# A joined tile of sparse weights, and modulation blocks spread unevenly over a projection

## The chip, the cores and the metric

The kernel runs on one core of a Trainium2 chip. The metric is the device time of one execution in microseconds (us). Engines are named as in the profile: PE is TensorE's matmul, PEld its weight load, DVE is VectorE, ACT is ScalarE, POOL is GpSimd, SP is SyncE, which issues the DMAs.

## The reference, cut to what matters

The kernel computes three layers of a sequence model on 512 tokens (256 context, 256 latent) of width 1024. The change lies in the first, "even" mixer, whose features come out of one projection:

```python
gq, gk, gv, gg, mq, mk, mv, mo, mg = _split(h @ w_in, EVEN_SIZES)     # 256 256 512 512 512 512 512 512 16
log_a = [log_sigmoid((h @ a1[d]) @ a2[d] + ab[d]) / GLA_TAU for d in range(2)]      # a1[d]: 1024 x 16
qk = silu(dwconv1d(concat([mq, mk]), conv_w, conv_b))
gates = (mg + gate_b).reshape(bsz, t, 4, ML_HEADS)
'li_f': gates[:, :, 0], 'lf_f': log_sigmoid(gates[:, :, 1])
'li_b': gates[:, :, 2], 'lf_b': log_sigmoid(gates[:, :, 3])
```

`h` is the normalised and modulated input. The modulation is `silu(c) @ mod_w[layer] + mod_b[layer]`, 6 x 1024 values for each layer and each of two conditions. The decays `log_a` go into a gated linear attention (GLA), q, k, v and gates of the second kind into an mLSTM.

## The kernel before

**Weights.** All weights stream through one ring of 5 slots in SBUF. A block is 8 tiles of 128x128 f32, 512 KB. `STREAM` (L109) is the order of the blocks, and SP's queue loads them in that order (`load_weights`, L248): slot i is loaded again when block i-5 is released. A product block is split into a high part (ACT, L493) and a low part (DVE, L498), kept in 3 buffers each (`PARTS`); each tile product is then 3 matmuls. A part's buffer is free when PE has used it up, so ACT makes part e+3 when item e is done, and DVE follows.

**Modulation blocks** (`Modulator.block`, L761) are not multiplied on PE. DVE multiplies each with the two conditions and sums (L769, twice for each block); that also releases its ring slot. DVE does such a block just before the low part of the product block that follows it in `STREAM` (`low_parts`, L587). 28 of them, m16 to m43, lie in the stage at hand.

**The stage `even_in`** (`even_projection`, L1267) has 31 items, each a bank of 512 columns with 8 tiles, so one block for each item. Item 0 is the low-rank decay input (`low`, 32 of 128 columns used), 1 to 4 are gq and gk, 5 to 8 gv, 9 and 10 are the gates `li` and `lf` (8 of 128 columns used in each), 11 to 18 mq and mk with their convolution on DVE, 19 to 22 mv, 23 to 26 gg, 27 to 30 mo. The items of gv, mv and mo are rounds of four that share their blocks; items 0 to 2 run together. PE may use 4 banks for items, so item e+4 waits until ACT has emptied item e.

**Beside them** runs the GLA (`GlaSteps`, L1329), in the other 4 banks. Its steps are written as generators, one for each engine, and each `yield` names a tick, two for each item: an engine takes the step up when its own walk through the items comes to that tick. Every step stands in the engine's one order of instructions, so what it waits for holds up all that is behind it. The ticks:

```python
DECAYS, DIAGONAL, LEVELS, SPACING = 6, 11, 13, 4
SUMS, KEYS, STATES, OUTPUTS, END = 41, (44, 46), (48, 50, 52), (54, 56), 61
```

At DECAYS PE multiplies `low` with `a2` (L1461), DVE clamps the result (L1608), ACT takes absolute value, exponential and logarithm (L1550 to L1553), DVE joins them (L1614). ACT empties item 4 only behind that. Seven levels of 4 ticks follow: distances on PE (L1452), an exponential on ACT, factors on DVE, scores on PE (L1443), taken over by DVE (L1604). SUMS are the last distances. KEYS makes decayed keys. STATES sums three states on PE (L1508); DVE copies them (L1666) and steps them (L1669), and between does the mLSTM gates' sums and peaks (L1740, L1749), on which PE's transposes of the gates wait (L1766) by way of ACT (L1760). OUTPUTS multiplies (L1527), ACT squares (L1579), DVE reduces (L1680) and, at tick OUTPUTS[1]+3, scales (L1686). At END PE transposes (L1539) and DVE applies the gate (L1693). On an even tick of item e, DVE takes the step up behind item e's low parts, on the odd tick after them and any convolution. 12 idle matmuls on PE (`tail`) close the stage; a barrier follows.

Of the kernel before, what the change touches and what calls it, by code (L numbers as in the profile page):

```python
# [22 lines left out]
ACT = mybir.ActivationFunctionType  # L23
AX = mybir.AxisListType

P = 128
D = 1024
KD = D // P
# [8 lines left out]
KF = FF // P  # L37
# [4 lines left out]
MH, MD = 4, 128  # L42
# [18 lines left out]


SEGMENTS = [
    ("mod0", 48 * KD), ("mod1", 48 * KD), ("even_in", 31 * KD), ("even_out", 8 * 8), ("up0", 2 * KF * KD),
    ("down0", 8 * KF), ("ssd_in", 41 * KD), ("ssd_out", 8 * KI), ("up1", 2 * KF * KD), ("down1", 8 * KF),
    ("in2", 85 * KD), ("branch2", 8 * 4 * KB), ("out2", 8 * KD),
]
# [20 lines left out]
def spread_among(few, many):  # L88

    out, placed = [], 0  # L90
    for i, b in enumerate(many):
        while placed < len(few) * (i + 1) // len(many):
            out.append(few[placed])
            placed += 1
        out.append(b)
    return out
# [2 lines left out]
MOD_FIRST = 16  # L99
MOD_PE = 4  # L100
SQUARES_AT = 2
MOD_EVEN = 44
MOD_DOWN = 27
MOD_ODD = 42
# [2 lines left out]
MOD_SSD = 25  # L107

STREAM = spread_among(blocks_of("mod0")[:MOD_PE], blocks_of("mod0")[MOD_PE:MOD_FIRST]) + blocks_of("even_in")[:TOGETHER] \  # L109
    + spread_among(blocks_of("mod0")[MOD_FIRST:MOD_EVEN], blocks_of("even_in")[TOGETHER:]) \  # L110
    + blocks_of("even_out")[:TOGETHER] + spread_among(blocks_of("mod0")[MOD_EVEN:], blocks_of("even_out")[TOGETHER:]) \
    + blocks_of("up0") + blocks_of("down0")[:DOWN_FIRST] \
    + spread_among(blocks_of("mod1")[:MOD_DOWN], blocks_of("down0")[DOWN_FIRST:]) \
# [3 lines left out]
for _name in ("up1", "down1", "in2", "branch2", "out2"):  # L117
# [4 lines left out]

COLUMNS = [
    ("mod_b0", 48), ("mod_b1", 48), ("mix_g0", 8), ("mix_g1", 8), ("ffn_g0", 8), ("ffn_g1", 8), ("final_g", 8),
    ("conv_w0", 9 * 44), ("conv_w1", 9 * 44), ("conv_b0", 44), ("conv_b1", 44), ("low_one", 1),
    ("ml_conv_w", 24), ("ml_conv_b", 8), ("gla_norm", 4), ("ml_norm", 4), ("ml_li_b", 1), ("ml_lf_b", 1),
    ("ssd_conv_w", 72), ("ssd_conv_b", 24), ("ssd_d", 16), ("ssd_norm", 16), ("ssd_dt_b", 1), ("ssd_a_log", 1),
    ("norm2", 8), ("qn_a", 1), ("kn_a", 1), ("qn_c", 1), ("kn_c", 1), ("b_forget", 1), ("lru_conv_w", 16),
    ("lru_conv_b", 4), ("b_rg_a", 4), ("b_rg_x", 4), ("lam", 4), ("cmp_pos", 32),
# [997 lines left out]
def setup(K, modulator, f, a2):  # L1127


    nc = K.nc  # L1130
    filled, loads, tokens, ones, rooted = K.counts(5)
    sums = SumSquares(K, 0, False)
    on_tensor, blocks = blocks_of("mod0")[:MOD_PE], blocks_of("mod0")[MOD_PE:MOD_FIRST]
    modulator.plan_tensor(on_tensor)
    modulator.plan(blocks)

    with nc.Block() as block:  # L1137
        @block.gpsimd
        def _(pool):
            link = Link(pool, filled)  # L1140
            for i, v in enumerate((EPS, 1.0, 0.0)):
                link(pool.memset(K.small[:, i:i + 1], v))
            pool.memset(K.ones[:], 1.0).then_inc(*ones.up())
            for a, v in ((K.ident, 0.0), (K.tri_f, 1.0), (K.tri_b, 1.0)):
                link(pool.memset(a[:], v))
            link(pool.affine_select(out=K.ident[:], in_=K.ident[:], compare_op=ALU.not_equal, fill=1.0, base=0,
                                    pattern=[[-1, P]], channel_multiplier=1))
            link(pool.affine_select(out=K.tri_f[:], in_=K.tri_f[:], compare_op=ALU.is_ge, fill=0.0, base=0,
                                    pattern=[[1, P]], channel_multiplier=-1))
            link(pool.affine_select(out=K.tri_b[:], in_=K.tri_b[:], compare_op=ALU.is_ge, fill=0.0, base=0,  # L1150
                                    pattern=[[-1, P]], channel_multiplier=1))

        @block.sync
        def _(sync):
            modulator.load(sync)
            sync.dma_start(K.cols[:], K.dram["columns"]).then_inc(*loads.up(16))
            sync.dma_start(a2[0:49, :], K.dram["gla_a2"]).then_inc(*loads.up(16))
            load_weights(K, sync, 0)
            sync.dma_start(K.x[:], K.dram["tokens"]).then_inc(*tokens.up(16))
            load_weights(K, sync, MOD_FIRST)  # L1160
            sync.wait_ge(*tokens.at(16))
            sync.wait_ge(*loads.at(32))

        @block.scalar
        def _(act):
            modulator.silu(act)
            for k in range(KD):
                sums.square(act, k, tokens.at(16))
            act.wait_ge(*sums.summed.at(KD))
            rsqrt(act, Link(act, rooted), f["lf"], K.sum_squares(0), K.small[:, 0:1], 1.0 / D)  # L1170

        @block.tensor
        def _(pe):
            for b in on_tensor[:SQUARES_AT]:
                modulator.sum(pe, b)
            pe.wait_ge(*ones.at(1))
            for k in range(KD):
                sums.add(pe, k)
            for b in on_tensor[SQUARES_AT:]:
                modulator.sum(pe, b)  # L1180

        @block.vector
        def _(dve):
            for b in blocks:
                modulator.block(dve, PLACE[b], b)
            dve.wait_ge(*loads.at(16))
            modulator.end(dve, blocks)
            modulator.take_sums(dve, MOD_PE)
    K.stage_end()
# [77 lines left out]
def even_projection(K, f, modulator, a2, gate_buffers):  # L1267
# [15 lines left out]
            return act.activation(dest, bank[0:dest.shape[0], :], func, scale=scale)  # L1283
        return empty

    def biased(dest, m, bias):
        return lambda act, bank: act.activation(dest[0:m, :], bank[0:m, :], ACT.Identity,
                                                bias=K.col(bias, rows=slice(0, m)), scale=1.0)

    def tokens(empty):  # L1290
        nonlocal tile
        groups = token_products(K, tile, T, range(TT), GW)
        rounds.append([Item(g, empty(i)) for i, g in enumerate(groups)])
        tile += 4 * KD

    one(biased(f["low"], 49, "low_one"))
    for name, scale in (("gq", GK ** -0.5), ("gk", 1.0)):
        for j in range(2):
            one(put(f[name][:, j, :], ACT.Copy, scale))
    tokens(lambda i: put(f["gv"][:, i, :], ACT.Copy))  # L1300
    one(biased(f["li"], 36, "ml_li_b"))
    one(biased(f["lf"], 36, "ml_lf_b"))
    for name, base in (("mq", 0), ("mk", 4)):
        for j in range(4):
            c = base + j
# [10 lines left out]
        return empty  # L1316
    tokens(value)
    for j in range(4):
        one(put(f["gg"][:, j, :], ACT.Copy, after=gla.keys_ended))
    tokens(lambda i: put(f["mo"][:, i, :], ACT.Sigmoid, after=gla.outputs_made))  # L1320
    rows = [f[name][:, j, :] for name in ("mq", "mk") for j in range(4)] + [f["lf"], f["li"]]
    run_products(K, first_together(rounds), (modulator, blocks_of("mod0")[MOD_FIRST:MOD_EVEN]),
# [1 line left out]


CHUNK_ORDER = ([0, 1, 2, 3], [1, 0, 3, 2])


class GlaSteps(Beside):  # L1329
# [8 lines left out]

    BANK = 4
    DECAYS, DIAGONAL, LEVELS, SPACING = 6, 11, 13, 4  # L1340
    SUMS, KEYS, STATES, OUTPUTS, END = 41, (44, 46), (48, 50, 52), (54, 56), 61
    N_INTERVALS = 2 * GLEVELS

    def __init__(self, K, f, a2, gate_buffers):
# [31 lines left out]
    def all_scored(self):  # L1376
        return self.scored.at(GLEVELS + 1)

    def keys_ended(self):
        return self.keyed.at(2)  # L1380

    def outputs_made(self):
        return self.outs.at(2)
# [50 lines left out]
    def tensor_steps(self, pe):  # L1434
# [22 lines left out]
        pe.wait_ge(*self.emptied(0))  # L1457
        for c in range(TT):
            for d in range(2):
                r = slice(32 * d, 32 * d + 17)  # L1460
                mm = pe.matmul(K.bank[:, B + 2 * d + c // 2, 256 * (c % 2):256 * (c % 2) + 256],  # L1461
                               f["low"][r, c * P:c * P + P], self.a2[r, :], start=True, stop=True)
            mm.then_inc(*self.decayed.up())
# [78 lines left out]
    def scalar_steps(self, act):  # L1542
# [40 lines left out]
        act.wait_ge(*self.convs_finished)  # L1583
        for name in ("mq", "mk", "gg"):
            if name == "gg":
                act.wait_ge(*self.emptied(26))
            ins = act.activation(f[name], f[name], ACT.Silu)
        ins.then_inc(*self.silued.up())

# [117 lines left out]
class MlstmGates:  # L1707
# [18 lines left out]

    def logarithms(self, act):
        link, e = Link(act, self.step_a), self.e
        link(act.activation(e, self.lf, ACT.Abs))
        link(act.activation(e, e, ACT.Exp, scale=-1.0))  # L1730
        act.activation(e, e, ACT.Ln, bias=self.K.small[0:self.R, 1:2], scale=1.0).then_inc(*self.logged.up())
# [1692 lines left out]
def lay_out(v):  # L3424
    f32 = np.float32
    parts = {}
    for l in range(2):

        by_rows = v["mod_w"][l].reshape(KD, P, 48, P).transpose(2, 0, 3, 1)
        if l == 0:  # L3430
# [6 lines left out]
        parts[f"down{l}"] = [mixed_tiles(v["ffn_w_down"][l], DOWN_TOGETHER)]  # L3437
    w = v["even_w_in"][0]
    gq, gk, gv, gg, mq, mk, mv, mo, mg = np.split(w, np.cumsum([256, 256, 512, 512, 512, 512, 512, 512]), axis=1)
    small = np.zeros((D, 3, P), f32)  # L3440
    small[:, 0, 0:16], small[:, 0, 32:48] = v["gla_a1"][0, 0], v["gla_a1"][0, 1]
    small[:, 1, 0:4], small[:, 1, 32:36] = mg[:, 0:4], mg[:, 8:12]
    small[:, 2, 0:4], small[:, 2, 32:36] = mg[:, 4:8], mg[:, 12:16]
    parts["even_in"] = [feature_tiles(small[:, 0]), feature_tiles(gq), feature_tiles(gk), token_tiles(gv),
                        feature_tiles(small[:, 1]), feature_tiles(small[:, 2]), feature_tiles(mq), feature_tiles(mk),
                        token_tiles(mv), feature_tiles(gg), token_tiles(mo)]
    parts["even_out"] = [feature_tiles(v["even_w_out"][0])]
    a2 = np.zeros((49, 256), f32)
    a2[0:16], a2[32:48] = v["gla_a2"][0, 0], v["gla_a2"][0, 1]
    a2[16], a2[48] = v["gla_ab"][0, 0], v["gla_ab"][0, 1]  # L3450

    w = v["ssd_w_in"][0]
    parts["ssd_in"] = [feature_tiles(widened(w[:, SI + 3072:])), feature_tiles(w[:, SI:SI + 3072]), feature_tiles(w[:, 0:SI])]
# [34 lines left out]
        put(f"conv_w{l}", taps(v["ffn_conv_w"][l].reshape(9, 2 * FF)))  # L3488
        put(f"conv_b{l}", feature_columns(v["ffn_conv_b"][l]))
    put("final_g", feature_columns(v["final_norm_g"]))  # L3490
    cols[[16, 48], COL["low_one"]] = 1.0
    put("ml_conv_w", taps(v["ml_conv_w"][0]))
    put("ml_conv_b", feature_columns(v["ml_conv_b"][0]))
    put("gla_norm", feature_columns(v["gla_norm_g"][0]))
    put("ml_norm", feature_columns(v["ml_norm_g"][0]))
    gb = v["ml_gate_b"][0]
    for name, a in (("ml_li_b", 0), ("ml_lf_b", 4)):
        cols[0:4, COL[name]], cols[32:36, COL[name]] = gb[a:a + 4], gb[8 + a:12 + a]
    put("ssd_conv_w", taps(v["ssd_conv_w"][0]))
    put("ssd_conv_b", feature_columns(v["ssd_conv_b"][0]))  # L3500
    put("ssd_d", feature_columns(np.repeat(v["ssd_d"][0], SP)))
# [50 lines left out]
```

## Time and profile before

| | us |
|---|---|
| median of 3 runs | 1797.47 (1797.27 to 1798.88) |
| the profiled execution | 1799.98 |
| its span, first to last instruction | 1798.3 |
| the stage `even_in` within it | 44.4 to 304.5 |

Times in rows are us from the start of the span. A row of the timeline has start, duration, engine, line, operation, out<-in, shapes, how many were merged (x), and in brackets the idle time of that engine before it with what ended it. "Granted" is the TensorE clock as a share of 2.4 GHz; 0.50 is 1.2 GHz.

### The profile page before, as it was taken

What the parts mean: (1) busy time and instruction counts of PE and PEld (TensorE: products, weight loads), DVE (VectorE), ACT (ScalarE), POOL (GpSimd) and SP (SyncE); (2) the same over time, 40 slices, a digit from 0 to 9 for tenths busy, and PEclk for the clock granted to TensorE, in tenths of its full rate; (3) what the DMA queues carried; (4) which work ended last, traced back from release to release, by engine and by line L of the source; (5) the groups of instructions that cost most, each with busy time, mean ns of one, the idle gap of its engine ahead of it and who ended that gap; (6) DMA issues with size and microseconds to landing.
All of it is one profiled execution on the core that took longest, in us unless ns stands there. A gap on an engine that the chain in (4) does not pass through costs nothing. (4 is left out here: it accounts for less than half of the span.)

```text
span 1798.3 us, 26476 instructions
## 1 busy us (share of the span) xinstructions
PE 1698.9 (94%) x10222; PEld 1448.4 (81%) x10222; DVE 1345.1 (75%) x2521; ACT 847.9 (47%) x1476; POOL 55.4 (3%) x113
## 2 busy tenths in 40 slices
PE   4899999898999999999999998999998999999997
PEld 3788877676888888877788766988897988989997
DVE  6678884876999999968984678699965555765594
ACT  2623335635544443245553565333344467665541
POOL 0910000000000000000000000000000000000000
PEclk9999999999999999999999999999999999999998
DMA  8343441031222226733553333554555454344452
GB/s 318 119 152 125 127 132 51 29 112 70 94 94 94 94 94 220 236 129 129 174 167 119 117 100 113 182 158 152 153 188 178 147 172 151 129 127 134 140 166 81
DMA packets 70150, 245.90 MB, mean 137 GB/s; under 512 B 7951, under 2 KB 9480, under 8 KB 69768
## 3 DMA queue, kind: packets, MB, share of 16 engines
q1 hardware_dynamic: 68024, 241.52, 41.5%
q10 hardware_dynamic: 2000, 2.69, 0.5%
q8 instruction: 81, 1.33, 0.3%
q14 instruction: 45, 0.37, 0.1%
HBM read 242.80 MB, written 1.11 MB: 136 GB/s over the span
## 5 line engine op out<-in xcount | busy, mean ns | idle before, releaser
L462 PE MATMUL banks<-m,weights_high 128*128 128x256 f32 (+1 forms) x4336 | 1045.0, 334 | 31.3 <-DVE weights_low L498 24.7
L462 PEld LDWEIGHTS banks<-m,weights_high 128*128 128x128 f32 x4336 | 737.2, 192 | 124.9 <-issue 23.3
L462 PE MATMUL banks<-m,weights_low 128*128 128x256 f32 (+1 forms) x2168 | 716.8, 331 | 0.0
L498 DVE TENSOR_TENSOR weights_low<-weight_ring,weights_high 128x1024 fp32r<-128x1024 f32 x293 | 355.5, 1222 | 226.8 <-ACT weights_high L493 225.9
L462 PEld LDWEIGHTS banks<-m,weights_low 128*128 128x128 f32 x2168 | 415.4, 192 | 37.5
L493 ACT ACTIVATE weights_high<-weight_ring 128x1024 fp32r<-128x1024 f32 x293 | 309.0, 1057 | 233.2 <-PE banks L462 152.9
L630 DVE SCALAR_TENSOR_TENSOR m<-m,columns 128x189 f32<-128x189 f32 (+4 forms) x856 | 321.8, 450 | 24.9 <-ACT m L570 24.7
L769 DVE SCALAR_TENSOR_TENSOR m<-weight_ring,m 128x1024 bf16<-128x1024 f32 x184 | 225.1, 1223 | 18.0 <-DMA weight_ring<-in_weights 12.2
L569 ACT ACTIVATE m<-banks,columns 128x512 f32<-128x512 f32 (+1 forms) x120 | 83.2, 693 | 303.8 <-PE banks L462 303.7
L462 PE MATMUL banks<-m,weight_ring 128*128 128x256 f32 x704 | 152.1, 379 | 0.0
L462 PEld LDWEIGHTS banks<-m,weight_ring 128*128 128x128 f32 x704 | 133.7, 190 | 18.1
L462 PE MATMUL banks<-weights_high,m 128*128 128x512 f32 (+1 forms) x288 | 89.8, 387 | 5.0 <-ACT m L1283 3.6
L2622 ACT ACTIVATE m<-banks 128x256 f32<-128x256 f32 x74 | 28.6, 387 | 104.1 <-PE banks L462 104.0
L462 PEld LDWEIGHTS banks<-weights_high,m 128*128 128x128 f32 x288 | 53.9, 191 | 17.1 <-ACT m L1283 5.3
L570 ACT ACTIVATE m<-banks 128x512 f32<-128x512 f32 (+1 forms) x120 | 60.4, 503 | 0.0
L462 PE MATMUL banks<-weights_low,m 128*128 128x512 f32 (+1 forms) x144 | 55.1, 383 | 0.0
L424 PEld LDWEIGHTS banks<-tri_f,identity 128*128 128x128 f32 x260 | 34.8, 218 | 16.4 <-issue 14.8
L424 PE MATMUL banks<-tri_f,identity 128*128 128x128 f32 x260 | 36.4, 304 | 11.7 <-PEq L1137 5.5
L2452 DVE TENSOR_TENSOR m<-m 128x768 f32<-128x768 f32 x32 | 30.5, 953 | 14.9 <-ACT m L2531 14.9
L1200 DVE TENSOR_TENSOR m<-m 128x512 f32<-128x512 f32 (+1 forms) x44 | 24.5, 557 | 22.2 <-ACT m L570 21.9
L2936 POOL MEMSET m<- 128x128 f32 x1 | 0.2, 205 | 1148.4 <-POOLq L418 1148.4
L2529 ACT ACTIVATE m<-banks,m 128x256 f32<-128x256 f32 x64 | 31.3, 488 | 4.8 <-PE banks L2390 4.8
(395 smaller groups left out, 1580.2 us busy)
## 6 DMA issues: line engine op xcount, KB each, us to landing
weight_ring<-in_weights SPq DMA_DIRECT2D x433, 512.0 KB, 3.7
m<-entering SPq DMA_DIRECT2D x32, 256.0 KB, 3.3
x<-in_tokens SPq DMA_DIRECT2D x1, 2048.0 KB, 14.3
m<-in_cmp_w SPq DMA_DIRECT2D x1, 2048.0 KB, 7.4
m<-in_cond SPq DMA_DIRECT2D x2, 512.0 KB, 4.9
out<-x ACTq DMA_DIRECT2D x8, 128.0 KB, 1.9
columns<-in_columns SPq DMA_DIRECT2D x1, 633.0 KB
m<-in_rg_w ACTq DMA_DIRECT2D x1, 512.0 KB, 3.5
```

The lines of the kernel that those rows point to most:

```text
L424: pe.matmul(K.bank[:, bank, 0:P], K.ident[:], K.tri_f[:], start=True, stop=True)
L462: mm = pe.matmul(out, lhsT, rhs, start=p.start and i == 0, stop=p.stop and i == len(passes) - 1)
L493: act.activation(w_hi[:, g % PARTS, :], K.ring[:, place % RING, :], ACT.Copy).then_inc(*K.high_done.up())
L498: dve.tensor_tensor(w_lo[:, g % PARTS, :], K.ring[:, PLACE[PRODUCT_BLOCKS[g]] % RING, :], w_hi[:, g % PARTS, :].bitcast(F32), ALU.subtract ...
L569: act.activation(acc[:, i % ACC, 0:c.n], bank[:, 0:c.n], ACT.Identity, bias=c.bias, scale=c.centre)
L570: act.activation(raw[:, i % RAW, 0:c.n], bank[:, 0:c.n], ACT.Copy).then_inc(*free_act.up())
L630: ins = dve.scalar_tensor_tensor(o, shift(raw[:, i % RAW, 0:c.n]), w, o, ALU.mult, ALU.add)
L769: dve.scalar_tensor_tensor(self.unread, K.ring[:, place % RING, :], 1.0, self.cond[:, c, :], ALU.mult, ALU.mult, accum_out=K.mod[:, layer, ...
L1200: return dve.tensor_tensor(g, a, g, ALU.mult)
L2452: dve.tensor_tensor(w, w, mid(cb[:, g % 2, d, :], 2), ALU.mult).then_inc(*weighted.up())
L2529: act.activation(w[:, 0:LAT], K.bank[:, LONG + i % 2, e * LAT:e * LAT + LAT], ACT.Exp, bias=dcol[:, SOURCE + sa, r:r + 1], scale=1.0)
L2622: act.activation(dest, bank[:, 0:LAT], func_of[func], scale=scale))])
```

## The change

One joined tile column (item 0) replaces the three sparse ones: in each direction's 32 columns, 4 of `li` and 16 of the low rank, and from column 64 on 4 of `lf` for each direction. So the stage has 29 items and blocks: gv stays at 5 to 8, the convolutions are 9 to 16, mv 17 to 20, gg 21 to 24, mo 25 to 28. Item 0 is emptied by three instructions; `lf`'s bias is added later, at KEYS[0]+1. The 28 modulation blocks are spread in three stretches: m16 to m23 before product blocks 3 to 6 (two before each), m24 to m33 among blocks 7 to 20, m34 to m43 among blocks 21 to 28. In the last stretch two stand before blocks 24 and 28, one before each other. The ticks of the levels keep their places 13, 17, ... 37. The later ticks move up.

```diff
-    ("mod0", 48 * KD), ("mod1", 48 * KD), ("even_in", 31 * KD), ...
+    ("mod0", 48 * KD), ("mod1", 48 * KD), ("even_in", 29 * KD), ...
+MOD_LEVELS, EVEN_LEVELS = 24, 7
+MOD_STATES, EVEN_STATES = 34, 21
-    + spread_among(blocks_of("mod0")[MOD_FIRST:MOD_EVEN], blocks_of("even_in")[TOGETHER:]) \
+    + spread_among(blocks_of("mod0")[MOD_FIRST:MOD_LEVELS], blocks_of("even_in")[TOGETHER:EVEN_LEVELS]) \
+    + spread_among(blocks_of("mod0")[MOD_LEVELS:MOD_STATES], blocks_of("even_in")[EVEN_LEVELS:EVEN_STATES]) \
+    + spread_among(blocks_of("mod0")[MOD_STATES:MOD_EVEN], blocks_of("even_in")[EVEN_STATES:]) \
...
+    def first_rows(act, bank):
+        for name, m in (("low", LOW_ROWS), ("li", MlstmGates.R)):
+            act.activation(f[name][0:m, :], bank[0:m, :], ACT.Identity, bias=K.col("first_b", rows=slice(0, m)), scale=1.0)
+        return act.activation(f["lf"][0:MlstmGates.R, :], bank[64:64 + MlstmGates.R, :], ACT.Copy)
+
-    one(biased(f["low"], 49, "low_one"))
+    one(first_rows)
...
-    one(biased(f["li"], 36, "ml_li_b"))
-    one(biased(f["lf"], 36, "ml_lf_b"))
...
-        one(put(f["gg"][:, j, :], ACT.Copy, after=gla.keys_ended))
+        one(put(f["gg"][:, j, :], ACT.Copy, after=lambda j=j: gla.keys_ended(j)))
...
-    SUMS, KEYS, STATES, OUTPUTS, END = 41, (44, 46), (48, 50, 52), (54, 56), 61
+    SUMS, KEYS, STATES, OUTPUTS, END = 41, (42, 45), (47, 48, 50), (51, 53), 57
...
-    def keys_ended(self):
-        return self.keyed.at(2)
+    def keys_ended(self, row):
+        return self.keyed.at(1 + row // 2)
...
-                act.wait_ge(*self.emptied(26))
+                act.wait_ge(*self.emptied(24))
...
+        link(act.activation(self.lf, self.lf, ACT.Identity, bias=self.K.col("ml_lf_b", rows=slice(0, self.R)), scale=1.0))
```

The rest of the diff lays out the joined tile, `a2` (53 rows instead of 49, `LOW_ROWS`) and the bias columns on the host.

## Rows read from the trace of the kernel before

**Rows 1.** The page: busy us, share of the span, instructions.
```profile
PE 1698.9 (94%) x10222; PEld 1448.4 (81%) x10222; DVE 1345.1 (75%) x2521; ACT 847.9 (47%) x1476; POOL 55.4 (3%) x113
```

**Rows 2.** Windows of the stage: length, busy of each engine, granted clock, DMA share, GB/s.
```profile
87.80:220.00 132.20, 131.76 (x864) 112.38 (x864) 108.18 (x138) 45.90 (x52) 8.15 (x8) 0.99 0.41 133
220.00:304.50 84.50, 81.54 (x472) 67.12 (x472) 56.53 (x89) 35.50 (x44) 2.01 (x5) 1.00 0.33 105
```

**Rows 3.** Timeline of PE in the opening of the stage.
```profile
70.81 0.73 PE L462 MATMUL banks<-m,weights_high 128*128 128x512 f32 x2 [1.63 <-DVE weights_low L498]
...
76.25 0.40 PE L462 MATMUL banks<-m,weights_low 128*128 128x512 f32 x1
...
83.77 0.39 PE L462 MATMUL banks<-m,weights_low 128*128 128x512 f32 x1
87.77 0.70 PE L462 MATMUL banks<-weights_high,m 128*128 128x512 f32 x1 [3.61 <-ACT m L1283]
```

**Rows 4.** Timeline of DVE in the opening of the stage.
```profile
69.52 1.23 DVE L498 TENSOR_TENSOR weights_low<-weight_ring,weights_high 128x1024 fp32r<-128x1024 f32 x1 [6.80 <-ACT weights_high L493]
70.67 1.26 DVE L769 SCALAR_TENSOR_TENSOR m<-weight_ring,m 128x1024 bf16<-128x1024 f32 x1
...
73.12 1.25 DVE L498 TENSOR_TENSOR weights_low<-weight_ring,weights_high 128x1024 fp32r<-128x1024 f32 x1
...
76.73 1.25 DVE L498 TENSOR_TENSOR weights_low<-weight_ring,weights_high 128x1024 fp32r<-128x1024 f32 x1
77.90 2.28 DVE L1608 TENSOR_SCALAR m<-banks 128x2048 f32<-128x2048 f32 x1
86.11 2.40 DVE L1614 SCALAR_TENSOR_TENSOR m<-m 128x1024 f32<-128x1024 f32 x2 [5.93 <-ACT m L1553]
```

**Rows 5.** Timeline of ACT in the opening of the stage.
```profile
67.86 0.68 ACT L1287 ACTIVATE m<-banks,columns 49x512 f32<-49x512 f32 x1 [8.44 <-PE banks L462]
68.44 1.05 ACT L493 ACTIVATE weights_high<-weight_ring 128x1024 fp32r<-128x1024 f32 x1
69.39 0.58 ACT L1283 ACTIVATE m<-banks 128x512 f32<-128x512 f32 x1
...
86.93 0.58 ACT L1283 ACTIVATE m<-banks 128x512 f32<-128x512 f32 x1
```

**Rows 6.** Windows around two pauses of PE.
```profile
84.40:87.80 3.40, 0.04 (x1) 0.07 (x1) 1.69 (x2) 3.40 (x4) 3.13 (x10) 1.00 0.00 0
87.80:91.30 3.50, 3.50 (x9) 2.73 (x10) 3.46 (x6) 0.66 (x1) 3.36 (x4) 0.51 0.00 0
...
39.00:44.40 5.40, 0.00 (x0) 0.00 (x0) 3.33 (x8) 0.00 (x0) 0.00 (x0) 0.60 1.00 401
44.40:50.20 5.80, 5.76 (x27) 5.79 (x28) 5.76 (x9) 5.78 (x9) 5.58 (x6) 0.50 0.57 201
```

**Rows 7.** Timeline of PE behind the levels.
```profile
222.14 1.95 PE L1452 MATMUL banks<-tri_b,m 128*128 128x128 f32 x16
...
247.50 1.09 PE L1508 MATMUL banks<-m 128*64 128x128 f32 x16
...
269.75 0.60 PE L1527 MATMUL banks<-m 128*128 128x128 f32 x4
...
298.25 1.91 PE L1539 MATMUL banks<-identity,m 128*128 128x128 f32 x16
301.53 2.94 PE L424 MATMUL banks<-tri_f,identity 128*128 128x128 f32 x24 [1.38 <-ACT m L1283]
```

**Rows 8.** Timeline of DVE behind the levels.
```profile
248.71 0.88 DVE L1666 COPY m<-banks 128x128 f32<-128x128 f32 x4 [0.69 <-PE banks L1508]
...
266.75 1.11 DVE L1669 SCALAR_TENSOR_TENSOR m<-m,banks 128x128 f32<-128x128 f32 x4
...
289.86 2.47 DVE L1686 TENSOR_TENSOR m<-banks,m 128x512 f32<-128x512 f32 x4
...
299.60 1.23 DVE L498 TENSOR_TENSOR weights_low<-weight_ring,weights_high 128x1024 fp32r<-128x1024 f32 x1 [1.44 <-ACT weights_high L493]
```

**Rows 9.** Timeline of ACT at the end of the stage.
```profile
298.51 1.06 ACT L493 ACTIVATE weights_high<-weight_ring 128x1024 fp32r<-128x1024 f32 x1 [1.60 <-PE banks L462]
```

More of the change, by code:

```diff
@@ L63 @@
 SEGMENTS = [
-    ("mod0", 48 * KD), ("mod1", 48 * KD), ("even_in", 31 * KD), ("even_out", 8 * 8), ("up0", 2 * KF * KD),
+    ("mod0", 48 * KD), ("mod1", 48 * KD), ("even_in", 29 * KD), ("even_out", 8 * 8), ("up0", 2 * KF * KD),
     ("down0", 8 * KF), ("ssd_in", 41 * KD), ("ssd_out", 8 * KI), ("up1", 2 * KF * KD), ("down1", 8 * KF),
@@ L124 @@
     ("mod_b0", 48), ("mod_b1", 48), ("mix_g0", 8), ("mix_g1", 8), ("ffn_g0", 8), ("ffn_g1", 8), ("final_g", 8),
-    ("conv_w0", 9 * 44), ("conv_w1", 9 * 44), ("conv_b0", 44), ("conv_b1", 44), ("low_one", 1),
-    ("ml_conv_w", 24), ("ml_conv_b", 8), ("gla_norm", 4), ("ml_norm", 4), ("ml_li_b", 1), ("ml_lf_b", 1),
+    ("conv_w0", 9 * 44), ("conv_w1", 9 * 44), ("conv_b0", 44), ("conv_b1", 44), ("first_b", 1),
+    ("ml_conv_w", 24), ("ml_conv_b", 8), ("gla_norm", 4), ("ml_norm", 4), ("ml_lf_b", 1),
     ("ssd_conv_w", 72), ("ssd_conv_b", 24), ("ssd_d", 16), ("ssd_norm", 16), ("ssd_dt_b", 1), ("ssd_a_log", 1),
@@ L1156, in _ @@
             sync.dma_start(K.cols[:], K.dram["columns"]).then_inc(*loads.up(16))
-            sync.dma_start(a2[0:49, :], K.dram["gla_a2"]).then_inc(*loads.up(16))
+            sync.dma_start(a2[0:LOW_ROWS, :], K.dram["gla_a2"]).then_inc(*loads.up(16))
             load_weights(K, sync, 0)
@@ L1284, in put @@
         return empty
-    def biased(dest, m, bias):
-        return lambda act, bank: act.activation(dest[0:m, :], bank[0:m, :], ACT.Identity,
-                                                bias=K.col(bias, rows=slice(0, m)), scale=1.0)
     def tokens(empty):
@@ L1326 @@
 CHUNK_ORDER = ([0, 1, 2, 3], [1, 0, 3, 2])
+LOW_AT, LOW_ONE = MH, MH + 16
+LOW_ROWS = 32 + LOW_ONE + 1
 class GlaSteps(Beside):
@@ L1459, in tensor_steps @@
             for d in range(2):
-                r = slice(32 * d, 32 * d + 17)
+                r = slice(32 * d, 32 * d + LOW_ONE + 1)
                 mm = pe.matmul(K.bank[:, B + 2 * d + c // 2, 256 * (c % 2):256 * (c % 2) + 256],
@@ L3439, in lay_out @@
     gq, gk, gv, gg, mq, mk, mv, mo, mg = np.split(w, np.cumsum([256, 256, 512, 512, 512, 512, 512, 512]), axis=1)
[L3440 to L3446, printed above, removed]
+    small = np.zeros((D, P), f32)
+    for d in range(2):
+        small[:, 32 * d:32 * d + MH] = mg[:, 8 * d:8 * d + 4]
+        small[:, 32 * d + LOW_AT:32 * d + LOW_ONE] = v["gla_a1"][0, d]
+        small[:, 64 + 32 * d:64 + 32 * d + MH] = mg[:, 8 * d + 4:8 * d + 8]
+    parts["even_in"] = [feature_tiles(small), feature_tiles(gq), feature_tiles(gk), token_tiles(gv), feature_tiles(mq),
+                        feature_tiles(mk), token_tiles(mv), feature_tiles(gg), token_tiles(mo)]
     parts["even_out"] = [feature_tiles(v["even_w_out"][0])]
-    a2 = np.zeros((49, 256), f32)
-    a2[0:16], a2[32:48] = v["gla_a2"][0, 0], v["gla_a2"][0, 1]
-    a2[16], a2[48] = v["gla_ab"][0, 0], v["gla_ab"][0, 1]
+    a2 = np.zeros((LOW_ROWS, 256), f32)
+    for d in range(2):
+        a2[32 * d + LOW_AT:32 * d + LOW_ONE], a2[32 * d + LOW_ONE] = v["gla_a2"][0, d], v["gla_ab"][0, d]
     w = v["ssd_w_in"][0]
@@ L3490, in lay_out @@
     put("final_g", feature_columns(v["final_norm_g"]))
-    cols[[16, 48], COL["low_one"]] = 1.0
     put("ml_conv_w", taps(v["ml_conv_w"][0]))
@@ L3496, in lay_out @@
     gb = v["ml_gate_b"][0]
-    for name, a in (("ml_li_b", 0), ("ml_lf_b", 4)):
-        cols[0:4, COL[name]], cols[32:36, COL[name]] = gb[a:a + 4], gb[8 + a:12 + a]
+    for d in range(2):
+        cols[32 * d + LOW_ONE, COL["first_b"]] = 1.0
+        cols[32 * d:32 * d + 4, COL["first_b"]], cols[32 * d:32 * d + 4, COL["ml_lf_b"]] = gb[8 * d:8 * d + 4], gb[8 * d + 4:8 * d + 8]
     put("ssd_conv_w", taps(v["ssd_conv_w"][0]))
```

## The prediction

> **What bounds the kernel now.** First the page's busy times [rows 1]: TensorE is busy for 94% of the span and VectorE for 75%, so TensorE is the first suspect. An average says little of one stage, so next come the windows over the stage that changes, the projection `even_in`, which runs from 44.4 to 304.5 us. From 87.8 to 220 us TensorE is busy for 131.76 of 132.2 us; from 220 to 304.5 it has 3 us of gaps [rows 2]. In the opening the timelines show it held up twice: 1.63 us for a low part, 3.61 us for a bank that ScalarE has to empty [rows 3]. So there are three regimes: an opening bound by a chain over VectorE and ScalarE, a long middle bound by TensorE, and an ending where both are close. Each edit has to be priced in its regime.
>
> **The removed tiles.** Items 9 and 10 of `even_in` go: 2 items of 8 tiles with 3 matmuls each, 48 matmuls. Matmuls stand 0.228 us apart (33 of them from 76.25 to 83.77 us [rows 3]), so an item is 5.47 us and the two are 10.9 us. They cannot be taken off the middle. The levels keep their 4 half items each and run from tick 13 to 41 before and after, so there TensorE has the same work: 0. All that goes lies between tick 41 and the end, where 20 ticks become 16. The low parts for these blocks (2 of about 1.2 us on VectorE, 2 of 1.05 us on ScalarE) go too; ScalarE's two emptyings move into the first item.
>
> [...]
>
> **The opening: +6.0 us.** VectorE runs in the order of its program: before part 3 stands block m16, before part 4 m17, before part 5 m18, and only then at tick 6 comes the clamp of the decays (L1608). After the change two blocks stand before each of parts 3 to 6.
> - The second block before part 3 costs nothing: VectorE sat idle 6.80 us before that part [rows 4], and a block is 2.45 us (70.67 to 73.12 [rows 4]).
> - The blocks before parts 4 and 5 have no such cover: parts and blocks follow one another without a gap up to L1608 [rows 4]. Two more blocks are +4.9 us.
> - The first item is now emptied by three instructions before ScalarE makes high part 3: another like L1287, which holds ScalarE for 0.58 us (67.86 to 68.44), and a copy like L1283's of about 0.5 us [rows 5]. Nothing covers that, since TensorE waits for part 3: +1.1 us.
> - L1608 thus starts at 83.9 instead of 77.90 us. Behind it on VectorE and ScalarE hang absolute value, exponential, logarithm, high part 6 and the emptying of item 4 at 86.93 us, and TensorE's next round waits for that bank [rows 3, 5]. It would resume at 93.8 instead of 87.77 us. TensorE would start item 3 at 71.9 us (1.1 later than in [rows 3]), need 5.5 us for it and 2 for the decays, and so want part 4 at 79.5 and part 5 at 85.1; they are done at 78 and 83.9, so the bank is the one wait that counts. The extra blocks' data land in time: the ring slot of part 5 is freed by m18 at 74.2 us, and VectorE wants that part only at 82.8.
> - Bounds: 0 if all of it were covered, +6.0 if none. I take +6.0, since the rows show a chain without gaps.
>
> **The clock: +0.7 us.** TensorE's pause grows from 3.6 to 8.6 us. After 3.6 us of idleness the clock went to 1.2 GHz as work resumed and stayed for 3.5 us (granted 0.51), which costs about 1.7 us; after the 5.4 us pause ahead of the stage it stood at 1.2 GHz for some 5.8 us of work [rows 6]. I take 5 us at half clock, 2.5 us lost, 0.7 more than before; the bounds are -1.7 and +3.4 (10 us at half).
>
> **Middle: 0.** After the opening VectorE has 10 blocks beside 14 items instead of 14. It wasn't late there (TensorE's gaps are 0.4 us in 132 [rows 2]), so four blocks fewer save nothing. Bounds: -0.4 and 0.
>
> **The ending: -3.9 us**, in four pieces.
> - From the last distances (their end at 224.09) to the first state sums (end 248.59 [rows 7]) TensorE had 3.5 items between, now 3: -2.7 us. The chains of the keys inside are short against the 16 us of products left, so I put no wait there; the nearest bound above is the 0.89 and less that single waits cost in this stretch (3 us of gaps in all [rows 2]).
> - From the first state sums to the first outputs. TensorE had 72 product matmuls there and now has 48, 5.5 us less. But VectorE works through one uninterrupted chain before the outputs may start: copies, gate sums, block and part, state step, peaks, block and part, state step, from 248.71 to 266.75 + 1.11 = 267.86 us [rows 8]. That is 19.2 us, and it is the same after the change. Before, the outputs started at 269.75, 21.2 us after the state sums [rows 7]; after, they can't before 19.3. So -1.9 us instead of -5.5: VectorE becomes the bound, and TensorE shows about 2.8 us before the gates' transposes (L1766) and 2.0 us before the outputs (L1527).
> - From there to the last product 3 items instead of 3.5: -2.7 us.
> - The tail. Before, the scaling (L1686, 2.47 us) was at tick 59, done before the last item ended (292.3 against 298.3), and transposes and idle matmuls ended at 301.53 + 2.94 = 304.47 us [rows 7, 8], 6.1 us after the last product. Now it stands at tick 56, an even tick of the last item, and VectorE comes to it only behind the last two low parts. The last of these waits for TensorE to release its buffer with the last product. After that product come high part 1.1 (as at 298.51 [rows 9]), low part 1.2 [rows 8], scaling 2.5, transposes 1.9, idle matmuls 2.9 us: 9.6 us against 6.1, **+3.5 us**. Bounds: 0, if TensorE were later than I think and the parts come early, and +3.5.
>
> Sum: 6.0 - 2.7 - 1.9 - 2.7 + 3.5 = +2.2 us, with the clock +2.9. The profiled execution took 1799.98 us (span 1798.3 and 1.7 around it), so its like would take 1802.9. It is 2.5 us above the median of the runs, 1797.47; from the median the forecast is **1800.4 us**. The gain of the removed tiles is given back in three places. Two blocks fewer to load (1 MB), one column less of bias and four rows more of `a2` lie under other work: 0, for the DMA engines are busy for 0.33 to 0.41 of this stretch [rows 2]. `lf`'s bias, one more instruction of ScalarE of about 0.6 us, falls where ScalarE is busy for 35.5 of 84.5 us: 0. Later stages keep their code.
>
> **Rivals.**
> - The clock decides (slower, 1803.1). A pause of 8.6 us leaves TensorE at 1.2 GHz for 10 us instead of 3.5. For it: after the pause ahead of the stage, the half clock held through idle and work together for about 10 us [rows 6]. Against: the matmuls that follow are dense. +2.2 + 3.4 = +5.6 us. It decides from about 6 us at half clock on.
> - The opening is covered (1794.7). If the extra blocks before parts 4 and 5 ran in gaps, L1608 would come 1.1 us later only: 1.1 - 3.9 = -2.8 us. For it: VectorE has 6.80 and then 8 us of idle time around there [rows 4]. Against: both gaps lie outside the three items in question.
> - TensorE alone counts (faster, 1786.6). All 10.9 us come out, as the 94% suggest. It needs opening, VectorE's chain and tail all hidden. For it speaks the 3 us of gaps in the last 84.5 us; against it the chain of 19.2 us, which does not shrink.
>
> **Chances.** A measurement tells about 0.2%, 3.6 us, from no change. My forecast has 0.50: 0.38 within the bound, 0.12 slower, as terms of 1 us either way would carry it over. The clock rival has 0.22 (0.20 slower, 0.02 within), the covered opening 0.13 (0.10 within, 0.03 faster), TensorE alone 0.10 (faster), and something that I don't see 0.05 (0.03 faster, 0.02 slower). That is 0.16 faster, 0.50 same, 0.34 slower. The range 1793.0 to 1804.5 reaches over the covered opening and the clock rival and leaves the third out.
>
> **What would show it.** L1608 near 83.9 us and TensorE resuming near 93.8; the levels at the same distances as now; waits of 2 to 3 us before L1766 and near 2 us before L1527, both on VectorE's account; the scaling of the outputs after the last low part, and the next stage starting near 307 us instead of 304.8. I am wrong if TensorE resumes before 90 us, or if no new wait shows after tick 41, or if the stage ends more than 3 us away from that.

## The result, and the profile after

The changed kernel is slower: 1807.15 us median (1797.89 to 1812.45, 20 runs) against 1797.34 us (1791.02 to 1801.18, 20 runs), ratio 1.0054, 95% interval 1.0042 to 1.0066. That is +9.8 us; 1800.4 us was forecast, and the median lies above the stated range of 1793.0 to 1804.5. The profiled execution took 1809.41 us (span 1807.7). Lines above 460 have moved by 4 to 6: L466 was L462, L1613 L1608, L1532 L1527, L1544 L1539, L1691 L1686.

Its stage `even_in` runs from 46.35 to 316.45 us, 270.1 us against 260.0. It starts 1.9 us later, a difference that lies ahead of it in the setup stage, and the stages behind it took 2.6 us less; no experiment looks into either. All times below count from the stage's start where they are written with a plus.

First the timeline of DVE in the opening, which answers to [rows 4]:

```profile
72.51 1.23 DVE L502 TENSOR_TENSOR weights_low<-weight_ring,weights_high 128x1024 fp32r<-128x1024 f32 x1 [5.25 <-ACT weights_high L497]
...
78.78 1.25 DVE L502 TENSOR_TENSOR weights_low<-weight_ring,weights_high 128x1024 fp32r<-128x1024 f32 x1
...
85.07 1.25 DVE L502 TENSOR_TENSOR weights_low<-weight_ring,weights_high 128x1024 fp32r<-128x1024 f32 x1
86.24 2.28 DVE L1613 TENSOR_SCALAR m<-banks 128x2048 f32<-128x2048 f32 x1
94.44 2.41 DVE L1619 SCALAR_TENSOR_TENSOR m<-m 128x1024 f32<-128x1024 f32 x2 [5.92 <-ACT m L1558]
```

Between two low parts (parts 3, 4 and 5 are the three shown) now lie 6.3 us instead of 3.6, and the clamp (L1613) comes at +39.9 instead of +33.5 us. The first item's emptying, on ACT:

```profile
69.67 1.26 ACT L1298 ACTIVATE m<-banks,columns 53x512 f32<-53x512 f32 x2 [8.34 <-PE banks L466]
70.94 0.59 ACT L1299 ACTIVATE m<-banks 36x512 f32<-36x512 f32 x1
71.43 1.04 ACT L497 ACTIVATE weights_high<-weight_ring 128x1024 fp32r<-128x1024 f32 x1
```

High part 3 comes 1.76 us behind the emptying's start instead of 0.58. On PE, the places where it waited or where a step starts; these answer to [rows 3, 7]:

```profile
73.79 0.74 PE L466 MATMUL banks<-m,weights_high 128*128 128x512 f32 x2 [2.80 <-DVE weights_low L502]
...
96.09 0.76 PE L466 MATMUL banks<-weights_high,m 128*128 128x512 f32 x1 [8.92 <-ACT m L1287]
...
230.60 1.95 PE L1457 MATMUL banks<-tri_b,m 128*128 128x128 f32 x16
...
253.21 1.09 PE L1513 MATMUL banks<-m 128*64 128x128 f32 x16
...
268.10 0.25 PE L1772 MATMUL banks<-identity,m 36*128 36x36 f32 x1 [2.01 <-ACT m L1766]
...
273.64 1.09 PE L1532 MATMUL banks<-m 128*128 128x128 f32 x4 [1.89 <-DVE m L1674]
...
309.08 3.67 PE L1544 MATMUL banks<-identity,m 128*128 128x128 f32 x16 [4.86 <-DVE m L1691]
```

Every wait that was forecast is there: 8.92 us for the bank (8.6 forecast), 2.01 before the gates' transposes (2.8), 1.89 before the outputs (2.0), and the last transposes behind the scaling. But look at the durations: the first four matmuls of the outputs take 1.09 us where [rows 7] has 0.60, and the last transposes 3.67 us where it has 1.91. The windows show why. A row has start and end, length, busy time of PE, PEld, DVE, ACT and POOL with the number of instructions, granted clock, DMA share and GB/s:

```profile
273.60:284.00 10.40, 10.36 (x39) 7.99 (x40) 7.24 (x11) 1.09 (x2) 0.00 (x0) 0.51 0.68 233
304.30:314.70 10.40, 5.62 (x27) 5.62 (x28) 7.15 (x11) 4.41 (x6) 0.00 (x0) 0.68 0.00 0
```

TensorE ran at 1.2 GHz (granted 0.51) for 10 us from the outputs on, and again through the transposes and idle matmuls of the tail, which together take 2.7 us longer than before. The order of the tail, on DVE, answers to [rows 8]:

```profile
303.47 1.23 DVE L502 TENSOR_TENSOR weights_low<-weight_ring,weights_high 128x1024 fp32r<-128x1024 f32 x1 [8.40 <-ACT weights_high L497]
305.41 1.23 DVE L502 TENSOR_TENSOR weights_low<-weight_ring,weights_high 128x1024 fp32r<-128x1024 f32 x1 [0.71 <-ACT weights_high L497]
306.55 2.48 DVE L1691 TENSOR_TENSOR m<-banks,m 128x512 f32<-128x512 f32 x4
310.31 3.23 DVE L1698 SCALAR_TENSOR_TENSOR m<-banks,columns,m 128x512 f32<-128x512 f32 x4 [1.29 <-PE banks L1544]
```

Stretch by stretch, each length from the rows above, those in [rows 3, 7] and the last product's end (304.2 us, before 298.4):

| stretch | before | after | difference | forecast |
|---|---|---|---|---|
| stage start to PE's resumption | 43.3 | 49.7 | +6.4 | +6.0, clock +0.7 behind it |
| to the end of the last distances | 136.3 | 136.5 | +0.1 | 0 |
| to the end of the first state sums | 24.5 | 21.8 | -2.7 | -2.7 |
| to the first outputs | 21.2 | 19.3 | -1.9 | -1.9 |
| to the last product's end | 28.7 | 30.6 | **+1.9** | -2.7 |
| to the last idle matmul's end | 6.1 | 12.2 | **+6.1** | +3.5 |

Two stretches are off, by 4.6 and 2.6 us, 7.2 together, and both hold the half clock. The 20 executions of the changed kernel point the same way, though only for the kernel as a whole: those with a mean granted clock of 0.975 to 0.977 took 1811.8 to 1812.5 us, those at 0.982 1800.1 to 1800.7, the one at 0.984 1797.9. That says how much moves with the clock, not in which stage.

### The profile page after: what moved, and what is told of

The parts are those of the page before. It is cut to its first block and busy times, and to the rows that moved or that the text cites. A ratio compares the mean times of both kernels' runs of the same rounds, so it can differ in the third digit from the quotient of the medians.

```text
span 1807.7 us, 26371 instructions
## 1 busy us (share of the span) xinstructions
PE 1691.8 (94%) x10174; PEld 1441.1 (80%) x10174; DVE 1344.0 (74%) x2519; ACT 846.2 (47%) x1475; POOL 56.8 (3%) x113
## 5 line engine op out<-in xcount | busy, mean ns | idle before, releaser
L466 PE MATMUL banks<-m,weights_high 128*128 128x256 f32 (+1 forms) x4304 | 1032.6, 333 | 33.3 <-DVE weights_low L502 26.8
L466 PEld LDWEIGHTS banks<-m,weights_high 128*128 128x128 f32 x4304 | 728.1, 191 | 124.5 <-issue 24.4
L466 PE MATMUL banks<-m,weights_low 128*128 128x256 f32 (+1 forms) x2152 | 708.3, 329 | 0.0
L466 PEld LDWEIGHTS banks<-m,weights_low 128*128 128x128 f32 x2152 | 410.2, 191 | 38.5
L466 PE MATMUL banks<-m,weight_ring 128*128 128x256 f32 x704 | 152.1, 379 | 0.0
L466 PEld LDWEIGHTS banks<-m,weight_ring 128*128 128x128 f32 x704 | 133.7, 190 | 18.1
L466 PE MATMUL banks<-weights_high,m 128*128 128x512 f32 (+1 forms) x288 | 91.3, 392 | 10.3 <-ACT m L1287 9.8
L466 PEld LDWEIGHTS banks<-weights_high,m 128*128 128x128 f32 x288 | 54.6, 193 | 22.8 <-ACT m L1287 10.6
L466 PE MATMUL banks<-weights_low,m 128*128 128x512 f32 (+1 forms) x144 | 55.6, 386 | 0.0
L2458 DVE TENSOR_TENSOR m<-m 128x768 f32<-128x768 f32 x32 | 30.6, 955 | 15.1 <-ACT m L2537 15.1
```

What stands on the lines that cost most here:

```text
L466: mm = pe.matmul(out, lhsT, rhs, start=p.start and i == 0, stop=p.stop and i == len(passes) - 1)
L2458: dve.tensor_tensor(w, w, mid(cb[:, g % 2, d, :], 2), ALU.mult).then_inc(*weighted.up())
```

## The experiments

Ratios are to the kernel before, from executions taken beside each other; its medians were 1797.52 us for the first four edits, 1798.11 for the next three and 1796.05 for the last three. Lines added by an edit move those behind them: L1532 of the changed kernel is L1542 in the kernels with a written list.

The theory after this reading: my sum of work and waits holds, and what it lacks is TensorE at half clock behind the new waits of the ending. The rival: chains on VectorE and ScalarE are longer than I priced, and the clock is a bystander.

**The scaling one tick earlier** (changed kernel, `x3_scale_early`):

```diff
-        yield self.OUTPUTS[1] + 3
+        yield self.OUTPUTS[1] + 2
```

> The changed kernel with one tick moved: VectorE scales the outputs at OUTPUTS[1]+2 instead of +3, so ahead of the last two low parts. Clock theory (the time that my sum missed, about 7 us, is TensorE at 1.2 GHz after the new pauses of the ending): the pause of 4.9 us before the last transposes goes (to under 1.5 us), no half clock follows it, and from the last product to the last idle matmul it takes 6 to 6.5 us instead of 12.2; against the kernel before +3.5 to +4.5 us instead of +9.8. Work theory (VectorE's chains are longer than I priced, the clock is noise): only the 3.5 us of the order of steps come back, +6.3.

Measured 1800.97 us, ratio 1.0021 (1.0008 to 1.0033). The last lines of PE's timeline in the stage:

```profile
304.64 1.91 PE L1544 MATMUL banks<-identity,m 128*128 128x128 f32 x16
307.92 2.94 PE L428 MATMUL banks<-tri_f,identity 128*128 128x128 f32 x24 [1.37 <-ACT m L1287]
```

No pause before the transposes, full clock, and the tail is 6.1 us long again. Of 9.8 us, about 6 come back (0.54% less 0.21%); the profiles divide that into 3.5 by the order (a pause of 1.37 us instead of 4.86) and 2.7 by the clock, since one edit removes both. The waits of the chain stayed, with their half clock.

**Idle matmuls in the chain's two waits** (changed kernel, `x4_filled_waits`): 9 before `gates.turn`, 9 before the wait for `updated.at(12)`, each

```diff
+                    pe.matmul(K.bank[:, B, 0:P], K.ident[:], K.tri_f[:], start=True, stop=True)
```

> The changed kernel with 9 idle matmuls before the gates' transposes and 9 before the first outputs, so in the two new waits of TensorE; what the engines wait for stays. Clock theory: the waits stay in length (now filled), but the clock holds at 2.4 GHz through the outputs, which take 4.2 us instead of 7.4, and the products behind them lose nothing: 4 to 5 us back, +5 us against before. Work theory: nothing comes back, +9.8 or a little more, since the idle matmuls only add work.

Measured 1801.4 us, ratio 1.0023 (1.0013 to 1.0034). PE's timeline and a window from the outputs on:

```profile
270.60 2.17 PE L1524 MATMUL banks<-tri_f,identity 128*128 128x128 f32 x18
272.60 0.64 PE L1536 MATMUL banks<-m 128*128 128x128 f32 x4
```

```profile
272.60:283.00 10.40, 10.40 (x64) 8.33 (x62) 7.04 (x11) 1.45 (x3) 0.00 (x0) 1.00 0.67 225
```

The outputs start at +227.2 us as in the changed kernel (+227.3), so nothing was gained by work or waits; yet 64 matmuls run in a window that held 39, and from the outputs to the last product it takes 26.0 us instead of 30.6. The granted clock of the window is 1.00 instead of 0.51, and these 4.6 us are the clock. By the runs 5.6 us come back (0.54% less 0.23%), where the clock theory expected 4 to 5 and the rival nothing. The rival falls here. In the tail, which this edit leaves alone, the pause is again 4.86 us, but the idle matmuls take 2.84 us and not 3.90: the half clock behind the same pause was shorter this time.

**No modulation block in the chain** (changed kernel, `x5_chain_bare`). Here and in the edits below the three calls of `spread_among` give way to a written list: `with_blocks(counts)` puts counts[i] modulation blocks before product block i of `even_in`, and what is left behind the last. The changed kernel's own list, written so, is 0,0,0, 2,2,2,2, 0,1,1,0,1,1,1,0,1,1,0,1,1,1 and 1,1,1,2,1,1,1,2.

```diff
-    + spread_among(blocks_of("mod0")[MOD_FIRST:MOD_LEVELS], ...
-    + spread_among(blocks_of("mod0")[MOD_LEVELS:MOD_STATES], ...
-    + spread_among(blocks_of("mod0")[MOD_STATES:MOD_EVEN], ...
+COUNTS = [0]*3 + [2]*4 + [0,1,1,0,1,1,1,0,1,1,0,1,1,1] + [1,1,1,2,1,0,0,2]
+    + with_blocks(COUNTS) \
```

> The changed kernel with no modulation block before product blocks 26 and 27: VectorE's chain from the first state sums to the outputs loses two blocks (4.9 of 19.2 us); they stand behind block 28 instead. Clock theory and my chain: both new waits fall under 0.5 us, the clock holds at 2.4 GHz there, 3.9 us of waits and 4 to 5 us of half clock come back, so +1 to +2 us against before. Work theory (waits without the clock): 3.9 us come back, +5.9.

Measured 1799.33 us, ratio 1.0013 (1.0004 to 1.0023). The gates' transposes and the outputs start without an idle entry, at 266.20 and 269.66 us:

```profile
266.20 0.25 PE L1782 MATMUL banks<-identity,m 36*128 36x36 f32 x1
...
269.66 0.60 PE L1542 MATMUL banks<-m 128*128 128x128 f32 x4
```

The outputs come at +223.1 instead of +227.3 us and the last product ends at +249.1 instead of +257.9: 4.2 us of waits and 4.6 of half clock. The median is 1.8 us above the kernel before, the ratio says 2.3; +1 to +2 was expected. VectorE's chain was the bound between the state sums and the outputs, as forecast.

**One block before each part of the opening** (changed kernel, `x2_opening_even`):

```diff
+COUNTS = [0]*3 + [1]*4 + [1]*14 + [1,1,1,2,1,1,1,2]
```

> The changed kernel with one modulation block before each of parts 3 to 6 instead of two; 14 instead of 10 among blocks 7 to 20, and 10 behind as before the edit. Both theories: the clamp of the decays comes 4.9 us earlier, 35.0 us behind the stage's start instead of 39.9, TensorE's pause in the opening falls from 8.9 to about 4 us, +4.9 against before. If four blocks more under the levels hurt there, TensorE shows waits of over 1 us among the levels and the gain is smaller; I expect none.

Measured 1802.14 us, ratio 1.0017 (0.9997 to 1.0037), an interval that still holds no change and +6.7 us; +4.9 was expected. The clamp comes at +33.7 us (35.0 expected), TensorE's pause is 2.64 us (4 expected), the first state sums end at +202.21 instead of +207.95. Not all of these 5.7 us are the order of the two blocks. In this execution TensorE came to full clock sooner at the start of the stage (its 24 idle matmuls took 7.15 us instead of 8.27), which brought part 3 about 1 us forward, and behind the pause before item 3 it ran at half clock for some 3.4 us, which the changed kernel's profile doesn't show. The order itself is the distance between the low parts: 3.7 and 3.6 us instead of 6.3 and 6.3, so 5.3 us. PE shows no wait among the levels but one of 0.7 us before the last level's distances, which the changed kernel has too, so four blocks more under the levels are free. That is the opposite of what the spread assumes.

**The spread alone on the kernel before** (kernel before with its 31 product blocks, `x1_spread_alone`):

```diff
-    + spread_among(blocks_of("mod0")[MOD_FIRST:MOD_EVEN], blocks_of("even_in")[TOGETHER:]) \
+COUNTS = [0]*3 + [2]*4 + [0,1,1,0,1,1,1,0,1,1,0,1,1,1] + [1]*10
+    + with_blocks(COUNTS) \
```

> The kernel before with the uneven spread alone: 31 items, three sparse tiles, ticks as before; two modulation blocks before each of parts 3 to 6, ten among blocks 7 to 20, one before each of blocks 21 to 30. The opening theory: the clamp comes 4.9 us later (38.4 us behind the stage's start), TensorE's pause grows from 3.6 to 8.5 us, and all of it is lost, since TensorE has no slack behind it: +4.9 us, 1 us more or less by the clock. Rival (the spread is free in a kernel with the old ticks, for VectorE idles before and after): 0.

Measured 1802.07 us against 1798.11, ratio 1.0028 (1.0012 to 1.0044), so +5.0 us by the ratio and +4.0 by the medians. The pause is there:

```profile
92.58 0.76 PE L474 MATMUL banks<-weights_high,m 128*128 128x512 f32 x1 [8.83 <-ACT m L1295]
```

**None before parts 4 and 5** (changed kernel, `x7_opening_bare`):

```diff
+COUNTS = [0]*3 + [2,0,0,2] + [1]*14 + [1,1,1,2,1,1,1,2]
```

> The changed kernel with the blocks of the opening moved: two before part 3 (where VectorE idles), none before parts 4 and 5, two before part 6; 14 among blocks 7 to 20, ten behind. Chain theory: the clamp is no longer held up by VectorE but by TensorE's decay products, about 31 us behind the stage's start; TensorE's pause falls to 1.5 to 2.5 us, and the clock may hold: 7 to 9 us faster than the changed kernel, +1 to +3 against before. Rival (the pause is set by ScalarE's two microsecond steps and the bank, whatever VectorE does): the pause stays near 4 us, as with one block each: +4 to +5.

Measured 1800.64 us, ratio 1.0027 (1.0009 to 1.0045), +4.9 us by the ratio and +2.5 by the medians. The clamp comes at +33.1, not +31, and the pause is 2.64 us, exactly as with one block each. As the chain theory said, the clamp now waits for TensorE's decay products (2.21 us). But it no longer sets the pause. ScalarE's timeline shows what does:

```profile
82.30 0.60 ACT L1297 ACTIVATE m<-banks 128x512 f32<-128x512 f32 x1 [6.41 <-PE banks L476]
82.79 1.88 ACT L1565 ACTIVATE m<-banks 128x2048 f32<-128x2048 f32 x1
```

ScalarE stands idle until TensorE has finished item 3, empties its bank, and only then takes the absolute value (L1565), although the clamp was done at 81.65 us. With one block each it is the same (emptying at 82.51 after 6.50 us of idleness); in the changed kernel ScalarE waited 6.18 us for the clamp instead. So the rival of this expectation has it right: behind a clamp this early the pause follows from ScalarE's order of steps, whatever VectorE does, though at 2.6 us and not 4. In both executions item 3 ran at half clock behind its 2.80 and 2.89 us of pause, which put the whole chain back. The bare opening was worth 0.1 us over the even one in the profiles.

**All cures** (changed kernel, `x6_all`):

```diff
+COUNTS = [0]*3 + [2,0,0,2] + [1]*14 + [1,1,1,1,1,0,0,3]
...
-        yield self.OUTPUTS[1] + 3
+        yield self.OUTPUTS[1] + 2
```

> The joined tile with the three cures together: opening as in the kernel with bare parts 4 and 5, none before blocks 26 and 27 and the last ones behind block 28, scaling at OUTPUTS[1]+2. If opening, chain, order of the tail and clock add up: TensorE's only pauses of over 0.8 us in the stage are before part 3 (2.8), one of 2 us in the opening and the 0.9 before mo; from start to the last idle matmul 246 to 249 us instead of 260 (before) and 270 (changed); -12 us against before, 1785.5. If they hide one another, it stays above 1792.

Measured 1787.4 us against 1798.11, ratio 0.9947 (0.9929 to 0.9965): faster than both, if by 9.5 us and not by the 12 expected. The stage takes 249.4 us; the cures add up, for in the profiles the early scaling took 6.3 us off the changed kernel's 270.1, the bare chain 8.9 and the bare opening 5.9, which would leave 249.0. The lines of its tail:

```profile
290.10 1.91 PE L1554 MATMUL banks<-identity,m 128*128 128x128 f32 x16
293.38 2.94 PE L438 MATMUL banks<-tri_f,identity 128*128 128x128 f32 x24 [1.38 <-ACT m L1297]
```

**The clock by itself, three times.** `x9_before_filled` is the kernel before with 14 idle matmuls in its opening pause:

```diff
+        yield 9
+        pe.wait_ge(*self.emptied(1))
+        for _ in range(14):
+            pe.matmul(K.bank[:, 1, 0:P], K.ident[:], K.tri_f[:], start=True, stop=True)
```

`x10_early_filled` is `x4_filled_waits` with the early scaling, 10 idle matmuls more at `yield self.DECAYS - 1` and 32 at `yield 9`. `x8_all_filled` is `x6_all` with 10 and 9 in these two places.

> The kernel before with 14 idle matmuls in the opening's pause of 3.6 us, nothing else. Clock theory: the pause is filled, the clock doesn't fall there, 1.7 us come back in executions in which it fell: -1 to -2 us. Rival (the clock's fall after so short a pause is rare or costs nothing): 0.

Measured 1796.05 us against 1796.05, ratio 0.9998 (0.9988 to 1.0008). A miss of the clock theory, which expected 1 to 2 us: no gain is to be seen, though in its profile the clock held (granted 1.00 from 87.8 to 91.3 us, where [rows 6] has 0.51) and the stage took 258.5 us instead of 260.0. The interval of 1.8 us to either side can't tell a gain of this size from none.

> The changed kernel, scaling at OUTPUTS[1]+2, and idle matmuls in each new or longer pause: 10 before item 3, 32 before the round of gv, 9 before the gates' transposes, 9 before the outputs. All waits stay, only the clock is held. If my sum without the clock is right, what is left against before is +6.4 (opening) - 7.3 (ending) = -0.9, and about -1 to -2 more for the fall of the clock that the kernel before pays itself: 1795 to 1797. If the missing 7 us were waits, it stays at +3 or more.

Measured 1796.4 us against 1796.05, ratio 0.9993 (0.998 to 1.0006), -1.3 us. Expected were -0.9 without the fall of the clock that the kernel before pays, and -1.9 to -2.9 with it; the interval can't tell these apart, but it leaves out the +3 or more of the rival. All waits of the changed kernel are in it except that of the tail:

```profile
271.46 0.64 PE L1543 MATMUL banks<-m 128*128 128x128 f32 x4
...
297.27 1.91 PE L1555 MATMUL banks<-identity,m 128*128 128x128 f32 x16
300.55 2.94 PE L428 MATMUL banks<-tri_f,identity 128*128 128x128 f32 x24 [1.37 <-ACT m L1287]
```

The outputs start at +225.7, the stage ends at +257.7 instead of +270.1, where the kernel before has +260.0.

> The kernel with all cures and 10 idle matmuls in its 2.8 us pause before item 3 and 9 in the 2.7 us pause before the round of gv. Clock theory: no half clock from the stage's first products to its end, 2 to 3.5 us faster than without them, 1784.5. Rival (after pauses under 3 us the clock falls seldom): no difference, 1787.5.

Measured 1784.59 us (6 runs) against 1796.05, ratio 0.9933 (0.9918 to 0.9949). The stage takes 246.2 us. This is the fastest version; over the one without idle matmuls it gains 0.14%, less than the two intervals can separate, though in the profiles its stage is 3.2 us shorter, with the granted clock at 1.00 through the opening.

## Why the prediction was wrong

- **The opening, +6.0: right** (+6.4). The missing 0.4 us: the two extra blocks cost 5.3 us and not 4.9 (two blocks together take 5.13 us, 73.65 to 78.78, where one took 2.45), and the emptying of item 0 cost 1.2 us instead of 1.1. The stretch from the clamp to the bank kept its 9.9 us. The edit of one block each, and the spread alone, confirm the mechanism. One reading beside it was wrong, and only the rival of the covered opening used it: VectorE's second gap, given as 8 us, is the 5.93 us of [rows 4].
- **The removed tiles: right.** TensorE lost nothing in the middle (+0.1) and 2.7 us before the state sums.
- **VectorE's chain, -1.9 instead of -5.5: right** to 0.1 us, shown by taking its two blocks out.
- **The last items, -2.7: failed.** They took 1.9 us more. The step of the prediction that failed is "The clock: +0.7 us". I priced the clock at one pause only, the one that grew in the opening, and there it cost no more than before (3.5 us at half clock before, 3.6 after). I had forecast two new waits and a gap in the tail myself, and gave them only their own length. Behind the two waits the clock stood at 1.2 GHz for 10 us of full work, 4.6 us lost, and in the profile filling the two waits brought just that back.
- **The tail, +3.5: its order was right, its size not.** The 3.5 us came with a pause of 4.86 us, and the half clock added 2.7 us to transposes and idle matmuls.
- The rival "the clock decides" named the cause but put it in the opening, at +3.4 us. In the ending it cost 7.2, by the profile of the changed kernel.
- The distance from profile to median held only roughly: +9.4 us by the profiled executions, +9.8 by the medians.

With the clock held by idle matmuls and the tail in order, the changed kernel stands level with the one before, which is what the sum without the clock says (6.4 us more in the opening, 7.3 less in the ending). What stays open is the share of each fall in the median, since the clock falls at different places from one execution to the next: the profile of one execution of each kernel shows 7.2 us in the ending, while the spread of the runs (0.975 to 0.984 granted) covers 14.6 us. Open is too which of the two waits brought the clock down, for every edit filled or removed both.

## What to carry to other kernels

Price each new wait of TensorE twice: its length, and as a second case the work behind it at half clock; where a wait can't be removed, idle matmuls in it were free here (the outputs came at +227.2 us with them and +227.3 without). Work on a second engine is hidden only if it doesn't stand in that engine's order before a step for which TensorE waits: the same 28 blocks and one scaling, in another order, turned +0.54% into -0.53%. When a stage gets shorter by its busiest engine, look for the chain on the others that keeps its length, and take its optional work out.

## What the runs showed of the hardware

I had not expected that two waits as short as 2.01 and 1.89 us, with 3.7 us of work between them, would be followed by 10 us at 1.2 GHz, when a single pause of 3.61 us had been followed by 3.5 us [rows 6]. All four profiles in which these two waits are open (the changed kernel, the early scaling, the even and the bare opening) show half clock behind them. The pause of 2.8 us before item 3 is less regular: in the changed kernel and in `x4_filled_waits` the work behind it ran at full clock, in five other profiles at half.

After the pause of 8.92 us TensorE worked only about 3.6 us at half clock: most of the 10.3 us of half clock lay in the pause itself.

```profile
89.40:99.70 10.30, 3.61 (x9) 2.87 (x10) 5.10 (x7) 7.32 (x6) 9.28 (x25) 0.50 0.06 23
```

The longer pause thus left less slow work behind it than the two short ones did. Why is not settled by these runs.
